# A hybrid encoder step: the convolution's units are projected before the gate z, and the scan moves under z's units

## The reference, cut to what matters

```
proj = rms_norm(x) @ w_in                      # indexer, q/k/v of A and B, gate z, xbc, dt
o_a  = sparse attention, o_b = band attention
xbc  = silu(causal_dwconv(xbc));  x, B, C = split(xbc)
y, h_last = ssd_scan(x, dt, a, B, C, h0, block)
y    = y + d_skip * x
g    = y * silu(z);  o_c = g * rsqrt(mean(g*g) per group + eps) * gate_norm
x    = x + concat(o_a, o_b, o_c) @ w_out
x    = x + relu(rms_norm(x) @ w_up)**2 @ w_down
```

## Time and profile before

| | us |
|---|---|
| median of 3 runs (3259.09 to 3263.89) | 3259.41 |
| span of the profiled execution | 3258.3 |
| PE busy | 3122.3 (96%) |
| DVE busy | 1711.3 (53%) |
| ACT busy | 1151.3 (35%) |
| mean granted TensorE clock | 0.978 |

### The profile page before, as it was taken

The page is one execution under the profiler, slowest core; times in us unless marked ns, Lnnn a source line. Parts: engine busy times, 40 slices in busy tenths (PEclk is TensorE's granted clock), DMA queues, the critical chain, the costliest instruction groups (busy, mean ns, idle before and its releaser), DMA issues.

```text
span 3258.3 us, 54928 instructions
## 1 busy us (share of the span) xinstructions
PE 3122.3 (96%) x20829; PEld 3064.7 (94%) x20829; DVE 1711.3 (53%) x2135; ACT 1151.3 (35%) x1376; POOL 135.7 (4%) x115
## 2 busy tenths in 40 slices
PE   6999999889999999999989999997999999999997
PEld 5899999689999999999989999986999999999997
DVE  5574467665434444444455745586644444444444
ACT  4333443233333333233323435422332333332333
POOL 4000000010000000000010000000100000000001
PEclk8999999799999999999999999997999999999999
DMA  6444443145455454454434544522454544544542
GB/s 201 125 146 126 143 143 113 57 123 146 150 150 148 148 149 149 150 150 149 130 109 131 153 143 126 155 89 64 128 151 150 149 148 148 149 150 149 150 141 79
DMA packets 233884, 444.64 MB, mean 136 GB/s; under 512 B 23073, under 2 KB 23521, under 8 KB 233425
## 3 DMA queue, kind: packets, MB, share of 16 engines
q1 hardware_dynamic: 228320, 426.37, 43.5%
q0 software_dynamic: 5424, 16.43, 1.6%
HBM read 430.94 MB, written 12.85 MB: 136 GB/s over the span
## 4 chain that ended last, share of the span: by engine, by line
PE 63%; issue 28%; DVE 5%; DVEq 1%; ACT 1%; POOLq 1%; DMA 0%; ACTq 0%; SPq 0%
PE G L682 19%; PE G L683 19%; PE G L684 19%; DVE raw_parts L1344 2%; PE M L719 1%; PE M L957 1%; PE M L851 1%; PE M L905 1%; ACT X L1043 1%; POOLq L528 0%; PE M L959 0%; DVEq L1372 0%; DVE xT L1504 0%; PE M L796 0%; PE M L777 0%
## 5 line engine op out<-in xcount | busy, mean ns | idle before, releaser
L1344 DVE TENSOR_TENSOR raw_parts<-raw,whi 128x1024 fp32r<-128x1024 f32 (+1 forms) x816 | 1013.3, 1258 | 884.5 <-ACT whi L1078 866.8
L1078 ACT ACTIVATE whi<-raw 128x1024 fp32r<-128x1024 f32 (+1 forms) x816 | 850.2, 1045 | 1469.5 <-PE G L684 1429.4
L682 PE MATMUL G<-X_parts,whi 128*128 128x320 f32 x3840 | 1200.2, 313 | 37.7 <-DVE raw_parts L1344 35.9
L684 PE MATMUL G<-X_parts,raw_parts 128*128 128x320 f32 x3840 | 1189.0, 310 | 0.0
L683 PE MATMUL G<-X_parts,whi 128*128 128x320 f32 x3840 | 1188.8, 310 | 0.0
L682 PE MATMUL G<-U_parts,whi 128*128 128x320 f32 x2560 | 805.1, 314 | 40.8 <-DVE raw_parts L1344 27.5
L683 PE MATMUL G<-U_parts,whi 128*128 128x320 f32 x2560 | 799.4, 312 | 0.0
L684 PE MATMUL G<-U_parts,raw_parts 128*128 128x320 f32 x2560 | 799.0, 312 | 0.0
L682 PEld LDWEIGHTS G<-X_parts,whi 128*128 128x128 f32 x3840 | 723.2, 188 | 44.6 <-issue 31.8
L683 PEld LDWEIGHTS G<-X_parts,whi 128*128 128x128 f32 x3840 | 723.3, 188 | 0.4
L684 PEld LDWEIGHTS G<-X_parts,raw_parts 128*128 128x128 f32 x3840 | 723.0, 188 | 0.0
(11 more groups left out here) (270 smaller groups left out, 1354.5 us busy)
## 6 DMA issues: line engine op xcount, KB each, us to landing
raw<-in_w_up SPq DMA_DIRECT2D x256, 512.0 KB, 3.7
raw<-in_w_down SPq DMA_DIRECT2D x256, 512.0 KB, 3.6
raw<-in_w_in SPq DMA_DIRECT2D x224, 512.0 KB, 3.6
raw<-in_w_out SPq DMA_DIRECT2D x64, 512.0 KB, 3.6
U<-in_x_prompt SPq DMA_DIRECT2D x2, 1024.0 KB, 7.4
out_y_prompt<-U SPq DMA_DIRECT2D x8, 256.0 KB, 2.6
bias_ext<-XC POOLq DMA_DIRECT2D x2, 768.0 KB, 5.0
raw<-in_w_in SPq DMA_DIRECT2D x16, 80.0 KB, 2.0
```

What stands on the lines that cost most here:

```text
L682: pe.matmul(out, hi, xh, start=(i == 0 and k == 0), stop=False)
L684: mm = pe.matmul(out, lo, xh, start=False, stop=(c == part[1] - 1 and k == KC - 1))
L1078: act.activation(whi[:, c % 4, :, cols], raw[:, c, :, cols], ACT.Copy).then_inc(high_done.sem, 1)
L1344: dve.tensor_tensor(wlo[:, c, :, cols], raw[:, c, :, cols], whi[:, c % 4, :, cols].bitcast(F32), ALU.subtract)\
```

## The change

The four xbc units now stand ahead of the two z units. The scan begins at slot 111, with two steps in three slots; its last step is due at slot 129. The gate is due at slot 130, ahead of the last top half unit. The multiplication by z leaves the steps: `gated` writes its sum back over x in XC, and after the last tile's step of a group `gate_rows` multiplies z by all tokens of that group. The squares are taken group by group. The scan's buffers move from X to parts of U and MIX that are free by then; two products are made in place. `scan_free` takes the place of `x_free`, and two waits are added on DVE (for stored key rows ahead of the first xbc read-out, for the state's rows ahead of the gate).

```
-        ("z", COL_Z, 0), ("z", COL_Z + UNIT, 1),
         ("xbc", COL_XBC, 0), ("xbc", COL_XBC + UNIT, 1), ("xbc", COL_XBC + 2 * UNIT, 2),
-        ("xbc", COL_XBC + 3 * UNIT, 3)]
+        ("xbc", COL_XBC + 3 * UNIT, 3),
+        ("z", COL_Z, 0), ("z", COL_Z + UNIT, 1)]
...
-    at = SLOTS_PROJ + 3
+    at = after(Q_XBC) + 5
     due["last"] = due["cb"] = at
+    for k in range(3 * C_GROUPS):
+        due["y", k // C_GROUPS, k % C_GROUPS] = at + 2 + 3 * k // 2
     for t in range(3):
-        due["tile", t] = at + 5 * t
-        for g in range(C_GROUPS):
-            due["y", t, g] = at + 5 * t + g + (t < 1)
-        due["so", t] = at + 5 * t + 5
-    due["gate"] = at + 17
+        due["so", t] = due["tile", t + 1] = due["y", t, C_GROUPS - 1] + 1
+    due["gate"] = due["so", 2]
...
-                                out=YT[r, p, 0:n], in0=XC[r, kb, at:at + n], scalar=dskip[r, kb:kb + 1],
+                                out=XC[r, kb, at:at + n], in0=XC[r, kb, at:at + n], scalar=dskip[r, kb:kb + 1],
...
-                    dve.tensor_tensor(Z[:, 2 * g:2 * g + 2, o:o + n], Z[:, 2 * g:2 * g + 2, o:o + n], YT[:, :, 0:n], ALU.mult)
...
+                def gate_rows(g):
+                    if g == 0:
+                        dve.wait_ge(z_ready.sem, z_ready.at(l, 2))
+                    z2 = Z[:, 2 * g:2 * g + 2, :]
+                    for o, n, at in ((0, SEQ, CONV_AT[0]), (SEQ, DEC_SEQ, CONV_AT[2])):
+                        ins = dve.tensor_tensor(z2[:, :, o:o + n], z2[:, :, o:o + n], XC[:, 2 * g:2 * g + 2, at:at + n], ALU.mult)
+                    ins.then_inc(gz.sem, 1)
...
                 def gate():
+                    dve.wait_ge(so_ready.sem, so_ready.at(l, 2))
```

More of the change, by code:

```diff
@@ L83 @@
 Q_SMALL = [k for k, _, _ in PROJ].index("small")
+Q_XBC = [k for k, _, _ in PROJ].index("xbc") + 3
 R_IW = IDX_DIM
@@ L307, in trunk, with state, squares @@
              "b": (BQ, BK, BV, KCb, VCb, PBb, PTb, [stgb0, Uf[:, tail:tail + UNIT]])}
-    take = carve(Xf)
+    take = carve(Uf[:, 8 * TOK:16 * TOK])
     XD, XDD, BT = take([C_WIDTH]), take([C_WIDTH]), take([UNIT])
[L311 to L316, removed]
+    take = carve(Uf[:, 24 * TOK:32 * TOK])
+    EX, EB = take([2, UNIT]), take([2, UNIT])
+    ST0 = take([UNIT])
+    take = carve(MIX[:, 0:8, :].rearrange("p k t -> p (k t)"))
+    H0, SO, ST1 = take([8, P]), take([C_WIDTH]), take([UNIT])
+    def state(first, n):
+        half = (ST0, ST1)[first // UNIT]
+        return half[:, first % UNIT:first % UNIT + n]
+    def squares(g):
+        return XC[:, 2 * g:2 * g + 2, 0:TOK]
     GRMS = TB[:, 0:C_GROUPS * TOK].rearrange("p (g t) -> p g t", g=C_GROUPS)
@@ L372, in trunk @@
     cache_b_in = Count(nc, "cache_b_in", 3, step=16)
-    x_free = Count(nc, "x_region_free", 1)
+    scan_free = Count(nc, "scan_buffers_free", 1)
     relu_idx = Count(nc, "relu_idx", 24)
@@ L408, in trunk @@
     so_out = Count(nc, "state_rows_stored", 2, step=16)
-    gz = Count(nc, "gated", 1)
+    gz = Count(nc, "gated", 4)
     gsq = Count(nc, "gate_squares", 4)
@@ L622, in _ @@
                     store_rows(l, 6 * i + 2 * t + 1, X_ + "v", t, VTOK[:, t, :], v_out)
-            pool.wait_ge(x_free.sem, x_free.at(l, 1))
+            pool.wait_ge(scan_free.sem, scan_free.at(l, 1))
             apart(pool)
@@ L928, in gate @@
                         for b in range(2):
-                            mm = pe.matmul(mb(key)[:, 0:TOK], ones[:], SQZ[:, 2 * g + b, :], start=(b == 0), stop=(b == 1))
+                            mm = pe.matmul(mb(key)[:, 0:TOK], ones[:], squares(g)[:, b, :], start=(b == 0), stop=(b == 1))
                         done_filling(mm, key)
@@ L956, in mixers @@
                         out = mb(key)[:, 2 * p * n:2 * (p + 1) * n]
-                        mm = pe.matmul(out, XD[0:n, f:f + P], MM[0:n, k % 2, 2 * p * n:2 * (p + 1) * n], start=True, stop=(t == 0))
+                        mm = pe.matmul(out, XD[0:n, f:f + P], EX[0:n, k % 2, 2 * p * n:2 * (p + 1) * n], start=True, stop=(t == 0))
                         if t:
-                            mm = pe.matmul(out, ST[:, f:f + P], CTS[:, k % 2, 2 * p * n:2 * (p + 1) * n], start=False, stop=True)
+                            mm = pe.matmul(out, state(f, P), EB[:, k % 2, 2 * p * n:2 * (p + 1) * n], start=False, stop=True)
                     done_filling(mm, key)
@@ L972, in mixers @@
                             key = ("so", t, i)
-                            transposes(l, key, [(mb(key)[:, b * P:(b + 1) * P], ST[:, (4 * i + b) * P:(4 * i + b + 1) * P]) for b in range(4)])
+                            transposes(l, key, [(mb(key)[:, b * P:(b + 1) * P], state((4 * i + b) * P, P)) for b in range(4)])
                     if t < 2:
@@ L1208, in gate @@
                 def gate():
-                    act.wait_ge(gz.sem, gz.at(l, 1))
-                    for g in range(C_GROUPS):
-                        act.activation(SQZ[:, 2 * g:2 * g + 2, :], Z[:, 2 * g:2 * g + 2, :], ACT.Square).then_inc(gsq.sem, 1)
+                    square_gated(C_GROUPS - 1)
                     for g in range(C_GROUPS):
@@ L1218, in gate, with square_gated @@
                         act.drain().then_inc(grms.sem, 1)
+                def square_gated(g):
+                    act.wait_ge(gz.sem, gz.at(l, g + 1))
+                    act.activation(squares(g), Z[:, 2 * g:2 * g + 2, :], ACT.Square).then_inc(gsq.sem, 1)
                 decays(0, 0)
@@ L1225, in mixers @@
                         decays(*groups[k + 1])
+                    if t == 2 and g:
+                        square_gated(g - 1)
                     if g < C_GROUPS - 1:
@@ L1447, in read_out @@
                     xr = conv_rows()
+                    if half == 0:
+                        dve.wait_ge(rows_out[0].sem, rows_out[0].at(l, 2))
+                        dve.wait_ge(rows_out[1].sem, rows_out[1].at(l, 1))
                     dve.memset(xr[:, :, 0:CTX], 0.0)
@@ L1620, in mixers @@
                     mix_operand(j).then_inc(x_mix.sem, 1)
+                dve.drain().then_inc(scan_free.sem, 1)
                 yield due["dt1"]
@@ L1684, in weights @@
                     k, at, n = 4 * t + g, CONV_AT[t], TILES[t][1]
-                    e_, m_ = EX[0:n, k % 2, 0:HPG * n], MM[0:n, k % 2, 0:HPG * n]
-                    eb, ct = EB[:, k % 2, 0:HPG * n], CTS[:, k % 2, 0:HPG * n]
+                    e_ = EX[0:n, k % 2, 0:HPG * n]
+                    eb = EB[:, k % 2, 0:HPG * n]
                     dve.wait_ge(ex_ready.sem, ex_ready.at(l, k + 1))
@@ L1709, in tile @@
                             filled(dve, l, key)
-                            drained(dve.tensor_copy(ST[:, i * UNIT:(i + 1) * UNIT], mb(key)), key)
+                            drained(dve.tensor_copy(state(i * UNIT, UNIT), mb(key)), key)
                         dve.drain().then_inc(st_first.sem, 1)
@@ L1779, in mixers @@
                     gated(t, g)
+                    if t == 2:
+                        gate_rows(g)
                     if k + 1 < len(groups):
```

14 lines of the change are left out of this document (4 added, 10 removed).

## The result

The changed kernel took 3244.14 us (median of 4 runs, 3241.99 to 3247.79) against 3259.93 us for the kernel before (4 runs beside it). The ratio is 0.9948, with a 95% interval of 0.9936 to 0.9960: 0.5% faster. The span of the profiled execution fell from 3258.3 to 3243.9 us, by 14.4 us; the forecast was 14.2 us.

The account below looks back on a forecast made before the run. PE, busy for 96% of the 3258.3 us span, was taken as the bound. Losses of 15.4 + 2.5 + 1.5 + 3.9 = 23.3 us a layer against 30.4 us gave 3259.4 - 14.2 = 3245 us, range 3232 to 3262.

Parts of the forecast that it names:

- The gate: At the third top half unit's residual, behind DVE's whole gate: PE waits 15.4 us a layer.
- The residual behind a long step: At tile 2's second step, PE waits for DVE to free the lower bank pair: 2.5 us a layer.
- The steps: Two scan steps in three slots: 16.1 us in tile 0, 18.2 us in tile 1; single waits of 1.5 us a layer.
- The clock: Among tile 2's steps, half of three steps are followed by a half-clock chunk: 3.9 us lost a layer.
- rival A: The clock holds until the gate: losses 19.4 us a layer, 3237 us; chance 0.25.
- rival C: The clock falls at tile 2's transposes and stays down until the gate: losses 38.5 us a layer, 3276 us; chance 0.13.
- The rule of the Trainium skill: At the 28 transposes at slot 124: one more slow chunk, 2.6 us a layer, 5.2 us in time; left out.
- B: DVE is late by 0.6 us at every scan step, 7.1 us a layer: 3259 us; chance 0.20.
- costs nothing: Xbc read-outs and taps under mixer B, earlier state load, new DVE waits and in-place products: no cost.

Follow-up runs that it names:

- the old slots: The changed kernel with scan and gate at the due slots of the kernel before, the other edits kept: 3246.0 us, ratio 0.9953.
- the late step: The changed kernel with DVE's gate cut into four pieces, and tile 2's second step one slot later (127): 3211.7 us, ratio 0.9840.
- the gate in pieces: The changed kernel with DVE's gate cut into four pieces at slots 130, 131, 132 and 135: 3219.6 us, ratio 0.9873.

## Why the prediction was right, and what it missed

*The gate.* The term was 15.4 us, made of 4.5 + 19.6 - 8.7. Measured: from the state's transposes (601.62) to the first reciprocal (606.10) 4.48 us; from there to PE's restart at 625.66 19.56 us; PE had work until 625.66 - 15.18 = 610.48, 8.86 us. The wait is 15.18 us. This step was the prediction, and it held to 0.2 us because each piece was taken from a row of the kernel before and the order was read from the instructions.

*The residual behind a long step.* Forecast 2.5 us, measured 1.67 us. From DVE's start of the step (578.74) to PE's restart (584.71) it took 5.97 us, not 6.3 us; and PE's cover, to the end of its chunk at 584.71 - 1.67 = 583.04, was 4.3 us, not 3.8 us. The old product by z, which I had left in as a reserve, should have come out.

*The steps.* Two steps in three slots took 16.15 us in tile 0 (forecast 16.1) and 17.9 us in tile 1 (18.2). Of the 1.5 us of single waits only 0.17 us is in the rows, ahead of tile 2; the wait of 1.67 us at the scan's start stood in the kernel before as well and lay within its 4.7 us. What did not stand there before is the slow chunk behind it. It took 5.12 us (485.23 to 490.35), where the kernel before took 3.60 us, since the granted clock fell:

```profile
486.00:488.00 2.00, 2.00 (x9) 2.00 (x8) 1.90 (x3) 1.79 (x3) 0.00 (x0) 0.50 0.05 12
```

No term of the sum had these 1.6 us (1.2 us in the second layer).

*The clock.* Forecast 3.9 us. Among tile 2's steps one chunk a layer fell, not one and a half, and for part of its length: 575.68 - 570.42 = 5.26 us, 1.7 us above a dense one (1.4 us in the second layer). In tile 2 the time thus lay nearer to rival A; with the chunk at the scan's start the clock cost 3.3 us, near the forecast, but in another place. I had also read only half of the fall in the kernel before. Behind the step that ends the clock fell again, for the chunk from 613.16 to 619.21 (6.05 us):

```profile
614.00:616.00 2.00, 2.00 (x10) 2.00 (x9) 1.50 (x5) 0.00 (x0) 0.00 (x0) 0.50 0.00 0
```

So there were two slow chunks a layer and not one, and that the clock rose again was weaker ground against rival C than it seemed. The rule of the Trainium skill that I left out of the sum ("TensorE: Matmul & The Clock Gate", section "Part 4: PE-mode transpose": transposes do not count as busy as matmuls do) would have added a slow chunk a layer. The trace does not bear that out: the clock was 1.00 behind tile 2's transposes in the changed kernel too, until the first step's end, and the chunk behind that step was slow, in one of two layers, also with matmuls in their place.

*What I had not counted.* Behind the gate's wait PE restarts cold, and the first eleven matmuls lie 0.27 us apart instead of 0.15: 1.3 us within the stretch, which before fell outside it. And a step of tile 2 takes PE 579.26 - 575.68 = 3.58 us, where I had put 3.2 us as work, and the last one 2.3 us instead of 1.3 us: 2.1 us that the sum books as a loss. Together 15.2 + 1.7 + 0.2 + 1.7 + 1.3 + 2.1 = 22.2 us of the 23.4 us; the chunk at the scan's start adds 1.6 us, and tile 1's steps took about half a us less than booked. So the total agreed to 0.1 us, with a term of 15 us sized to 0.2 us and small ones that were off by 1 to 2 us each in both directions, and with the restart in one total and not in the other. That is luck on top of a right mechanism. The span has luck in it too: the two layers' stretches from slot 112 to the end of the first bottom chunk became 16.6 us shorter, and the work between them took 2.7 us longer (1430.5 against 1427.8 us). Other kernels with the scan in new slots took 1426 to 1431 us there, so nothing shows that the change costs this.

*Rivals.* B (DVE late at every step) and C (clock down until the gate) did not show: PE's waits among the steps are gone but for the two named, and the clock was back at 1.00 from 574.

*What it missed.* I asked what the new order costs, and never what the edits beside it are worth in the old order. I priced them as "costs nothing" or as a reserve. The runs show that in the old slots early squares and products by group bring as much as the whole change (3246.0 against 3244.1 us), and that the new place then adds about 2 us. The time was right because the losses in the new place were counted directly, whatever their cause. The statement that the placement saves 7 us a layer would have been wrong as an explanation: what it saves in waits, the wait behind the gate takes back (from slot 112 to the first bottom chunk PE idles for 19.2 us a layer before, and for 18.7 us after), and what is left is time at the low clock. With that wait removed, the kernel in the new slots is 26 us faster than the one in the old slots (3219.6 against 3246.0), and with the late step 34 us. That is not the worth of the place alone, since the gate in pieces was not run in the old slots. There PE waits for the gate's result for 13.8 us in two layers, and the cold restart behind it costs some 3.5 us; by these rows pieces could give back 17 us at most, and an estimated 9 us would stay for the place.

## What to carry to other kernels

When a stage moves under other work, look at what every engine's ordered queue puts behind it: here DVE's 19.6 us of gate stood ahead of a 0.8 us read-out that PE needed, and cutting the block into pieces was worth more than the move. A change of several edits needs each of them priced in the old order as well; two orders can lose the same time in different places. And when a predicted total fits, compare term by term before believing the explanation, busy time as well as waits: here the waits' sum hardly changed, and the clock made the difference.

## What the hardware showed unexpectedly

- The clock's fall among tile 2's steps is not a fixed property of the program. In the kernel with the gate in pieces the first layer had three slow chunks (5.14 us behind the scan's start, 5.25 and 6.09 us in tile 2), and the second layer, with the same instructions, none. Here are stretches of that execution at the same step in either layer:

```profile
572.00:574.00 2.00, 2.00 (x10) 2.00 (x10) 1.86 (x5) 0.00 (x0) 0.00 (x0) 0.60 0.00 0
...
2154.00:2156.00 2.00, 2.00 (x15) 1.78 (x13) 1.86 (x5) 0.00 (x0) 0.00 (x0) 1.00 0.00 0
```

- While PE stood idle behind the gate from 610.48, the granted clock stayed at 1.00 to about 614 and was at 0.50 from 616 until after the restart at 625.66:

```profile
612.00:614.00 2.00, 0.00 (x0) 0.00 (x0) 1.85 (x4) 0.00 (x0) 0.00 (x0) 1.00 0.75 248
...
616.00:618.00 2.00, 0.00 (x0) 0.00 (x0) 1.93 (x3) 0.00 (x0) 0.00 (x0) 0.50 0.00 0
```

- A transpose and a plain float32 matmul of the same shape with the identity do not cost the same: the 28 transposes ahead of tile 2 took 3.1 us (560.03 to 563.15), the 28 matmuls, which the trace shows as 56, took 6.5 us (559.34 to 565.87).
